# Rotary embedding of the second attention: the cosine product moved from VectorE to GpSimd

## The reference

```
def apply_rope(x, cos, sin):
    half = x.shape[-1] // 2
    x1, x2 = xf[..., :half], xf[..., half:]
    return jnp.concatenate([x1 * cos - x2 * sin, x2 * cos + x1 * sin], axis=-1)
...
    proj = h @ w_in[l]
    q_m, k_m, v_m, q_d, k_d, v_d, gate_m, gate_d = jnp.split(proj, IN_SPLITS, axis=-1)
    qm = apply_rope(to_heads(q_m, MOBA_HEADS, MOBA_HEAD_DIM), cos_m, sin_m)
    km = apply_rope(to_heads(k_m, MOBA_HEADS, MOBA_HEAD_DIM), cos_m, sin_m)
```

## Time and profile before

| | us |
|---|---|
| Three runs | 1062.47, 1062.64 (median), 1063.32 |
| The profiled execution, its own time | 1063.16 |
| Its span, first to last instruction | 1061.4 |
| Busy in the span: PE / DVE / ACT / POOL | 911.6 / 551.6 / 358.2 / 76.0 |

### The profile page before, as it was taken

The page is one execution under the profiler, slowest core; times in us unless marked ns, Lnnn a source line. Parts: engine busy times, 40 slices in busy tenths (PEclk is TensorE's granted clock), DMA queues, the critical chain, the costliest instruction groups (busy, mean ns, idle before and its releaser), DMA issues.

```text
span 1061.4 us, 19424 instructions
## 1 busy us (share of the span) xinstructions
PE 911.6 (86%) x8462; PEld 706.2 (67%) x8462; DVE 551.6 (52%) x1020; ACT 358.2 (34%) x698; POOL 76.0 (7%) x113
## 2 busy tenths in 40 slices
PE   9999999999999999999999998667655666657784
PEld 8787777489999888988989965334333343334442
DVE  4775688858888766798867643211112121211211
ACT  5710355246776536456553341000001010000002
POOL 3022710000000000331010000000000000000000
PEclk9999999999999999999999999988888887989878
DMA  9545453695554565876549899999999999999994
GB/s 350 164 165 185 143 190 120 219 286 170 160 174 174 202 233 190 267 233 215 179 148 387 350 386 426 430 427 430 426 431 427 429 428 429 430 427 429 426 431 200
DMA packets 76715, 316.21 MB, mean 298 GB/s; under 512 B 4087, under 2 KB 28064, under 8 KB 64208
## 3 DMA queue, kind: packets, MB, share of 16 engines
q1 hardware_dynamic: 71972, 302.24, 72.5%
q0 software_dynamic: 4512, 12.62, 4.0%
q10 hardware_dynamic: 140, 0.04, 0.0%
HBM read 311.72 MB, written 1.06 MB: 295 GB/s over the span
## 4 chain that ended last, share of the span: by engine, by line
PE 61%; DMA 25%; DVE 7%; ACT 3%; issue 3%; ACTq 0%; SPq 0%; POOL 0%; DVEq 0%
PE ps L486 59%; DMA w<-in_w_up 18%; DMA w<-in_w_down 4%; DMA w<-in_w_gate 3%; DVE sp L1940 1%; DMA rot<-q 1%; PE ps L612 1%; PE ps L2803 1%; DVE acc L1003 0%; ACT hts L2937 0%; DVE wr L680 0%; DVE w L1041 0%; ACTq L3200 0%; ACT sp L1931 0%; DVE q L2314 0%
## 5 line engine op out<-in xcount | busy, mean ns | idle before, releaser
L486 PE MATMUL ps<-w,xg 128*32 128x256 f32 x2016 | 156.5, 469 | 96.7 <-DMA w<-in_w_up 75.8
L486 PE MATMUL ps<-hb,sp 128*128 128x256 f32 x1824 | 224.4, 283 | 0.0
L486 PEld LDWEIGHTS ps<-hb,sp 128*128 128x128 f32 x1824 | 218.6, 188 | 3.0 <-issue 2.5
L486 PEld LDWEIGHTS ps<-w,xg 128*32 128x32 f32 x2016 | 83.3, 130 | 167.5 <-issue 143.6
L1940 DVE TENSOR_TENSOR sp<-w,sp 128x1024 fp32r<-128x1024 f32 x122 | 144.6, 1220 | 37.5 <-ACT sp L1931 37.4
L1931 ACT ACTIVATE sp<-w 128x1024 fp32r<-128x1024 f32 x122 | 122.3, 1052 | 46.0 <-PE ps L486 42.4
L3013 DVE TENSOR_TENSOR cst<-ps,cst 64x256 f32<-64x256 f32 x31 | 13.3, 428 | 214.6 <-ACT cst L2924 214.6
L2924 ACT ACTIVATE cst<-ps 64x256 f32<-64x256 f32 x31 | 11.7, 377 | 309.8 <-PE ps L486 309.8
L3039 DVE TENSOR_TENSOR ost<-ps,cst 32x256 f32<-32x256 f32 x120 | 50.5, 420 | 103.3 <-PE ps L486 100.5
L486 PE MATMUL ps<-w,hts 128*32 128x256 f32 x1024 | 63.6, 390 | 13.1 <-ACT hts L2937 10.3
L486 PE MATMUL ps<-sp,ab 128*128 128x512 f32 x264 | 61.7, 395 | 0.0
(11 more groups left out here) (430 smaller groups left out, 1304.7 us busy)
## 6 DMA issues: line engine op xcount, KB each, us to landing
w<-in_w_down SPq DMA_DIRECT2D x36, 2048.0 KB, 35.8
w<-in_w_gate SPq DMA_DIRECT2D x32, 2048.0 KB, 28.1
w<-in_w_up SPq DMA_DIRECT2D x31, 2048.0 KB, 33.1
w<-in_w_in SPq DMA_DIRECT2D x13, 2048.0 KB, 9.5
w<-in_w_up SPq DMA_DIRECT2D x22, 1024.0 KB, 7.6
w<-in_w_ada SPq DMA_DIRECT2D x8, 2048.0 KB, 8.7
w<-in_w_out SPq DMA_DIRECT2D x4, 2048.0 KB, 8.0
w<-in_w_ada POOLq DMA_DIRECT2D x8, 768.0 KB, 5.8
```

The source lines that it names most:

```text
L486: return q.eng.matmul(o, l, r, start=start, stop=stop, skip_group_check=True)
```

## The change

GpSimd does the cosine product in a new function `cos_gp`. It waits for the rotation of the half to have landed (the transfers read q, and the product overwrites it) and for its own last count in a semaphore. VectorE keeps the sine product and the sum, and the sum waits for both. The counts of `rope` go from three to two a half. The semaphore `u_z`, which two memsets used, is renamed `gp_fill` and counts the products too. On GpSimd the product of a half is written ahead of the rotation of the next.

```diff
+        def cos_gp(q, h):
+            r, qv = ROPES.index(h), v(q_half(h), 2)
+            q.wait_ge(s[f"rot{r % 2}"], 64 * (r // 2 + 1))
+            q.wait_ge(s["gp_fill"], 2 + r)
+            q.eng.tensor_tensor(qv, qv, bc(C["cos"].unsqueeze(1), [128, 2, 256]), MUL).then_inc(s["gp_fill"], 1)
...
@@ rotate_gp
             if r > 1:
-                q.wait_ge(s["rope"], 3 * r - 3)
+                q.wait_ge(s["rope"], 2 * r - 2)
...
@@ proj2_pe
-                    q.wait_ge(s["rope"], 12 if kind == "moba" else 24)
+                    q.wait_ge(s["rope"], 8 if kind == "moba" else 16)
...
@@ proj2_ve
                     e.tensor_tensor(rtv, rtv, sinb, MUL).then_inc(s["rope"], 1)
-                    e.tensor_tensor(qv, qv, cosb, MUL).then_inc(s["rope"], 1)
-                    q.wait_ge(s["rope"], 3 * r + 2)
+                    q.wait_ge(s["rope"], 2 * r + 1)
+                    q.wait_ge(s["gp_fill"], 3 + r)
                     e.tensor_tensor(qv, qv, rtv, ADD).then_inc(s["rope"], 1)
...
@@ gpsimd
             rotate_gp(q, 2)
             for n in range(6, 9):
                 ada_late_gp(q, n)
-                rotate_gp(q, 2 * n - 9)
-                rotate_gp(q, 2 * n - 8)
+                for h in (2 * n - 9, 2 * n - 8):
+                    cos_gp(q, h - 1)
+                    rotate_gp(q, h)
             ada_late_gp(q, 9)
+            cos_gp(q, 8)
             rotate_gp(q, 9)
+            cos_gp(q, 9)
```

More of the change, by code:

```diff
@@ L98 @@
         "r_ya", "r_yv", "r_n", "wo_mm", "x1",
-        "hi", "split", "half_mm", "u_z", "u_ev", "u_c", "u_v", "u_s", "a_hi", "a_lo", "dn_mm", "x_ffn", "q_ev", "rot0", "rot1", "rope",
+        "hi", "split", "half_mm", "gp_fill", "u_ev", "u_c", "u_v", "u_s", "a_hi", "a_lo", "dn_mm", "x_ffn", "q_ev", "rot0", "rot1", "rope",
         "od_sq", "mg_mm", "mg_v", "mg_hi", "mg_lo", "od_mm", "od_n", "od_hi", "od_lo", "o2_mm", "x_mix",
@@ L2012, in up_sc @@
                     q.wait_ge(s["half_mm"], j + 1)
-                    q.wait_ge(s["u_z"], 2)
+                    q.wait_ge(s["gp_fill"], 2)
                     q.wait_ge(s["a_lo"], i - 1)
@@ L2271, in proj2_ve @@
             e = q.eng
-            cosb = bc(C["cos"].unsqueeze(1), [128, 2, 256])
             sinb = bc(C["sin"].unsqueeze(1), [128, 2, 256])
@@ L3379, in _ @@
             for u in Uz:
-                e.memset(v(u, 4)[:, :, 0:2], 0.0).then_inc(s["u_z"], 1)
+                e.memset(v(u, 4)[:, :, 0:2], 0.0).then_inc(s["gp_fill"], 1)
             for n in range(6):
```

## The result

| kernel | runs | median us | ratio to before, 95% interval |
|---|---|---|---|
| before | 7 | 1062.64 | |
| changed | 7 | 1071.1 (1067.53 to 1073.12) | 1.0066 [1.0046, 1.0086] |
| changed, again (e8) | 4 | 1069.37 | 1.0057 [1.0037, 1.0077] |

Each ratio compares all runs of a kernel with the runs of the kernel before of the same session, not the medians of this column: in the first row the means are 1063.35 and 1070.37, and the partner of e8 is 11 runs of the kernel before with a median of 1064.28. The change makes the kernel slower by 0.66%, 7.0 us of 1062.6, with 4.9 to 9.1 in the interval. The forecast was 1066.5, 3.9 us slower, in a range that ends at 1071.0. Before plus 7.0 is 1069.7, inside it; the median alone, 1071.1, is 0.1 above its end. The profiled execution of the changed kernel took 1068.87 us, its span is 1067.1.

A forecast was written before the change was run, and what follows sets the result against it. It took the chain of waits through VectorE to bound this stretch, with at most 2.6 us to win. 1063.16 + 3.9 (4.6 late at half 5's sum, less 0.7) = 1067.1, and 0.5 lower gives 1066.5 us; range 1061.8 to 1071.0.

The forecast's parts named there:

- The queue is the cost, not the product: On GpSimd's in-order queue, each rotation waits behind the previous half's product, so two rotations are never under way together.
- The walk to the sum of half 5: From 440.24, four products, three rotations and the sum in series end at 465.3 instead of 460.72, 4.6 us late.
- 440.24, unchanged: Landing of half 2's rotation, where the serial steps begin; taken as unmoved because nothing ahead of it moves.
- That rotation and chunk are coupled: Weight chunks follow VectorE's splits behind a rope, so half 4's rotation meets no chunk: 3.4 us, against 7.1 beside one.
- From there to 491, -0.7 us: Three ropes, halves 6 to 8, give back 0.7 us (bounds 1.8 gained, 0.9 lost), leaving 3.9 us late at 491.
- GpSimd's rotations here roughly keep up with VectorE's spacing: For halves 6 to 8, up to 491, rotations of 3.4 to 7.1 us plus 1.7 each would about match VectorE.
- The clock: PE's granted clock should stay at 1.00; a single gap of 5 us was a small risk left in the range.
- One to one behind 491: Nothing after 491 gives the lateness back; the whole expert weight stream and its tail move with it.
- The size: Total slowdown of 3.9 us against the profiled execution, giving 1066.5 us as the forecast median.
- All slow: Rival: rotations of 7.1, 7.1 and 9.0 us end half 5's sum at 470.9; +9.5, 1072.1 us; chance 0.14.
- VectorE's saving wins: Rival: VectorE between 458 and 488 saves 0.61 a rope, up to 2.6 us; 1060.0 at best; chance 0.10.
- The rule on the shared port pair: Two-input VectorE instructions and GpSimd's SBUF reads exclude each other: product 1.94 us, four costing 1.0 us more than counted.

The follow-up runs named there:

- e8: The changed kernel run once more, unaltered, for a second trace; median 1069.37 us, ratio 1.0057 to the kernel before.
- experiment 2: Kernel before, all on VectorE, but each rotation is issued only when the previous half's rope is complete; 1074.4 us, ratio 1.0089.
- experiment 1: Changed kernel with GpSimd's queue reordered: rotations of halves 3 to 7 issued before the previous half's product; median 1066.05 us, ratio 1.0019.
- experiment 7: Four 2 MB weight chunks cut to 512 KB, in the changed kernel (ratio 1.0006) and in the kernel before (0.9991).
- experiment 3: Changed kernel with ten dummy matmuls on PE ahead of its wait for the rope, to hold the clock; ratio 1.0067.
- experiment 8: Kernel before with only the cosine products of halves 6 to 9 moved to GpSimd (ratio 0.9993), or left out altogether (0.9975).

## Why the prediction was right, and where it was off

- *The queue is the cost, not the product.* Right. Order alone gives the loss without any product (experiment 2), and undoing it takes most of it away (experiment 1).
- *The walk to the sum of half 5.* Right nearly step by step: rotations of 7.1, 3.4 and 7.1 us were forecast; measured from the rows above, to the start of the product, are 6.8, 3.4 and 7.9. Products 1.7, measured 1.8. The sum was to end at 465.3 and ended at 466.47, of which 1.4 us are the drift ahead of the changed code: 4.4 us late against 4.6. That it came so close is in part luck. "440.24, unchanged" was wrong: the rotation of half 2 took 6.6 us where it had taken 7.6, so the walk began 1.0 us earlier, and the longer rotation of half 5 (0.8) and the longer products (0.3) made up for it.
- *That rotation and chunk are coupled.* The short rotation of half 4 rested on the next chunk being released by the same rope. The second trace repeats it, and experiment 7 bears the coupling out for half 3, whose rotation fell from 6.8 us to 3.4 beside a small chunk.
- *From there to 491, -0.7 us.* This is the step that failed. "GpSimd's rotations here roughly keep up with VectorE's spacing" is wrong for half 7: issued at 470.30, behind `w_ada` and beside a chunk, it took 8.3 us, and VectorE waited 0.48 and then 1.26 us (rows above). Its softmax step at 484.66 was stretched to 1.11 us beside the product of half 8, where the same form takes 0.42 at 470.69. Instead of 0.7 gained, 0.7 was lost: 4.4 became 5.07.
- *The clock.* "The clock should not fall" was wrong, 0.50 for about 3 us. No price of it is seen (experiment 3).
- *One to one behind 491.* Right as far as traces tell: 508.8 and 508.05 us from the mark to the end, 508.85 in the second trace, and the weight stream 5.1 us late at its start, at 429 GB/s in both kernels (700 to 1000 us, and the same stretch 6 us later).
- *The size.* Forecast 3.9, traces 5.07 and 5.89, runs 7.0 [4.9, 9.1] and 6.1 [3.9, 8.2]. The stage explains 5 to 6. The 1.4 us ahead of the change are not its own: the matmuls between 232 and 300 us take 285 ns in that trace and 281 before, and again 282 in the second trace of the very same program, and 285 in two kernels of which neither has a product on GpSimd. A remainder of about 1 us is inside the intervals, and no run here explains it.
- *The rivals.* "All slow" did not occur, as the short rotation of half 4 is in both traces. "VectorE's saving wins" is seen only where nothing is chained, 0.4 us behind the sum of half 5 in the trace of experiment 8, against a bound of 2.6, and the runs do not tell it from nothing.
- *The rule on the shared port pair.* By the Trainium skill (SBUF — State Buffer, section "SBUF: two separate sides", on the port pair that VectorE and GpSimd share) the product would last 1.94 us where the sine product holds the pair first, an estimate from the rule and the single durations. Measured: 1.76 to 1.80 together, 1.28 alone, and in experiment 1 a sine product of 1.80 and 2.23. Direction and rough size agree, but not every row: the sine product of 2.23 us began 0.38 us ahead of GpSimd's product (452.27 and 452.65; spans on GpSimd are rough), and by the rule the one that begins first is not stretched. In size, the sum of four such products, 7.1 us, lies between the 6.8 I counted and the 7.8 by the rule.

## What to carry to other kernels

Before an instruction that waits for a transfer is put on a queue, look at what that queue issues next: if it is the next transfer, the overlap of two is gone, and each step costs issue + landing + work. Compare that sum with the pace that the consumer needs (here 5.7 us against steps of 8.4, 8.5 and 5.2 from one rotation to the next), and read the landing in the traffic it will meet, not the median. Here the product lost time where its result was awaited and the next transfer stood behind it; where the rotations kept their order and the first scores did not wait for it (experiment 8), it lost nothing, and won too little for the runs to tell.

## What the runs showed of the hardware

- A small transfer from SBUF to SBUF (64 KB) landed 1.9 us after its issue on DMA engines with little to do and up to 8 us beside a 2 MB load, whether GpSimd or ScalarE issued it (maxima 7.5 and 8.0 in the kernel before and the changed one, 7.0 and 7.1 with ScalarE).
- A 64 KB issue occupied GpSimd for 0.50 us and ScalarE for 0.61 (medians of 32).
- Two-input instructions of VectorE and GpSimd stretch each other: 0.69 became 1.80 and 2.23, 1.28 became 1.8.
- PE's granted clock fell to 0.50 behind a wait of 5 us, in the second trace during it, and was back at 0.98 some 4 us after PE resumed (the stretch from 470 to 472). In the trace of experiment 1, with a wait of 1.3 us, it stayed at 1.00.
- The same matmuls between 232 and 300 us, at a granted clock of 1.00, took 281 to 282 ns in eleven traces and 285 in three, which made 1.4 us of drift by 400 us in the trace of the changed kernel.
